# Conv taps and modulation rows shared out anew between the stages of a layer, and the last expert's activations turned on TensorE

## The reference

```python
mod = c_act @ w_ada[l] + b_ada[l]              # six rows of 1024
shift1, scale1, gate1, shift2, scale2, gate2 = split(mod, 6)
h = rms_norm(x) * (1 + scale1) + shift1
proj = h @ w_in[l]
attn_out = attention of 4 heads, 1024 x 1024 softmax each
conv_out = silu(layer_norm(conv of 31 taps over 512 channels (a * sigmoid(g))))
x = x + gate1 * (concat(attn_out, conv_out) @ w_out[l])
h2 = rms_norm(x) * (1 + scale2) + shift2
x = x + gate2 * expert_choice_ffn(h2)          # 16 experts, each takes 128 tokens
```

## Time and profile before

| | |
|---|---|
| median of 3 runs | 4063.68 us (4060.52 to 4064.96) |
| profiled execution | 4063.72 us, its span 4061.9 us |
| TensorE busy | 3778.4 us, 93% of the span |
| VectorE busy | 2656.0 us, 65% |
| ScalarE, GpSimd busy | 22%, 13% |
| mean granted TensorE clock | 0.971 of full speed |

### The profile page before, as it was taken

The page is one execution under the profiler, slowest core; times in us unless marked ns, Lnnn a source line. Parts: engine busy times, 40 slices in busy tenths (PEclk is TensorE's granted clock), DMA queues, the critical chain, the costliest instruction groups (busy, mean ns, idle before and its releaser), DMA issues. The chain is left out here.

```text
span 4061.9 us, 41680 instructions
## 1 busy us (share of the span) xinstructions
PE 3778.4 (93%) x16116; PEld 1723.8 (42%) x16116; DVE 2656.0 (65%) x3557; ACT 901.9 (22%) x1736; POOL 546.1 (13%) x415
## 2 busy tenths in 40 slices
PE   6989995999997998996999999799988999999998
PEld 3444442333333444443333333344476444444443
DVE  6779737888885588966688888445443253333676
ACT  2244321111111234421211111233243110000000
POOL 2000002121111000001111110000020022222541
PEclk8999997999998999998999999899998999999999
DMA  8210327999995631055799998311010111111454
GB/s 300 82 42 1 123 80 286 350 348 348 351 347 181 228 103 42 1 194 211 277 350 357 342 355 329 104 36 37 16 45 17 75 46 52 42 42 42 176 202 166
DMA packets 186964, 682.50 MB, mean 168 GB/s; under 512 B 16656, under 2 KB 80784, under 8 KB 137616
## 3 DMA queue, kind: packets, MB, share of 16 engines
q1 hardware_dynamic: 177264, 646.27, 42.4%
q0 software_dynamic: 9504, 33.56, 3.4%
HBM read 637.83 MB, written 41.94 MB: 167 GB/s over the span
## 5 line engine op out<-in xcount | busy, mean ns | idle before, releaser
L1724 PE MATMUL ps<-w_raw,h_act 128*64 128x512 f32 x2048 | 456.0, 598 | 6.2 <-ACT h_act L1829 6.2
L1777 PE MATMUL ps<-w_down,h_act 128*128 128x512 f32 x960 | 417.2, 592 | 0.6 <-DVE h_act L1945 0.6
L1724 PE MATMUL ps<-w_t,h_act 128*64 128x512 f32 x1536 | 342.0, 594 | 0.0
L3437 PE MATMUL ps<-h_act,arena_two 128*128 128x512 f32 x704 | 313.2, 592 | 1.8 <-ACT h_act L455 0.9
L983 DVE SCALAR_TENSOR_TENSOR y<-y,par_one 128x1024 f32<-128x1024 f32 x240 | 307.2, 1280 | 2.6
L1724 PEld LDWEIGHTS ps<-w_raw,h_act 128*64 128x64 f32 x2048 | 148.7, 138 | 300.1 <-issue 300.1
L1777 PEld LDWEIGHTS ps<-w_down,h_act 128*128 128x128 f32 x960 | 180.1, 190 | 217.6 <-issue 215.2
L3437 PE MATMUL ps<-arena_two 128*128 128x512 f32 x528 | 237.4, 592 | 0.0
L1945 DVE STREAM_TRANSPOSE h_act<-h_act 32x256 f32<-32x256 f32 x512 | 223.2, 436 | 20.6
L2279 PE MATMUL ps<-h_act,arena_two 128*128 128x512 f32 x544 | 235.4, 593 | 1.0 <-DVE h_act L466 1.0
L650 PE MATMUL ps<-h_act,arena_a 128*128 128x512 f32 x512 | 221.6, 593 | 4.5 <-DVE h_act L466 2.0
(11 more groups left out here) (487 smaller groups left out, 5830.8 us busy)
## 6 DMA issues: line engine op xcount, KB each, us to landing
w_raw<-in_w_gate SPq DMA_DIRECT2D x128, 1024.0 KB, 7.4
w_raw<-in_w_up SPq DMA_DIRECT2D x128, 1024.0 KB, 9.9
w_down<-in_w_down SPq DMA_DIRECT2D x128, 1024.0 KB, 8.2
arena_two<-in_ffn_w_down SPq DMA_DIRECT2D x44, 1024.0 KB, 4.9
arena_two<-in_ffn_w_up SPq DMA_DIRECT2D x22, 1024.0 KB, 5.1
arena_b<-in_w_ada SPq DMA_DIRECT2D x32, 512.0 KB, 5.3
arena_b<-in_w_ada_T SPq DMA_DIRECT2D x32, 512.0 KB, 4.4
arena_two<-in_w_in SPq DMA_DIRECT2D x21, 512.0 KB, 3.9
```

Source lines behind the costliest of these rows:

```text
L1724: last = nc.tensor.matmul(out[w * TOK:(w + 1) * TOK, :], left[:, k, :], right[:, w, k, :], start=begins and k == 0, stop=k == KH1 - 1, ski ...
L1777: last = nc.tensor.matmul(ps[:, 4 + i, :], hidT[:, k * P:(k + 1) * P], down[:, c, k % 2, i * HALF:(i + 1) * HALF], start=(k == 0), stop=(k ...
L3437: last = nc.tensor.matmul(ps[:, q % 8, :], left[:, k, :], right[k], start=k == 0, stop=k == KH - 1)
```

## The change

- Layer 1's rows 3 and 4 (16 pieces) are no longer computed in layer 1's `mix_one`, but in layer 0's `out_projection_one`, whose number of pieces rises from 16 to 32. There `fills["rows"]` is 14 for both layers; in layer 0 it was 16, and the other places of `fills`, 18 pieces in all, were not reached. Layer 1's `mix_one` keeps the gate rows of its own and of the second block (32 pieces in place of 48).
- In `mix_one` of both layers the fills ahead of the attention units have 92 places in place of 80. With 32 pieces these hold 60 taps (before: 48 in layer 0, 32 in layer 1).
- In the attention units the first five take one tap each, and the others `left // (N_UNITS - u)`, with six taps held back until after the last unit.
- In the last expert of each layer VectorE doesn't turn the activations. TensorE turns them with eight 128 x 128 transposes in two groups of four into two PSUM banks, ScalarE copies each bank to `hidT`, and `last_down` takes k = 4 to 7 first.

```diff
+FIRST_UNITS, LAST_TAPS = 5, 6
...
                 gate(0)
-                fill(20)
+                fill(21)
                 gate(1)
+                fill(5)
                 for t in range(QT):
                     scale_latents(t)
-                    fill(3)
+                    fill(3 + t % 2)
...
-                fill(16)
+                fill(18)
                 gate(2)
                 fill(20)
...
-                    left = n_taps - done[0]
-                    some = -(-left // (N_UNITS - u))
+                    left = n_taps - LAST_TAPS - done[0]
+                    some = 1 if u < FIRST_UNITS else left // (N_UNITS - u)
                     tap_some(min(1, some))
...
                     tap_some(max(0, some - 1))
+                tap_some(LAST_TAPS)
...
-    fills = {"rows": 16 if l == 0 else 14, ("added", 0): 2, ("added", 1): 2, ("scaled", 0): 2, ("scaled", 1): 2, ("scored", 3): 2,
+    fills = {"rows": 14, ("added", 0): 2, ("added", 1): 2, ("scaled", 0): 2, ("scaled", 1): 2, ("scored", 3): 2,
...
+LAST_ORDER = (4, 5, 6, 7, 0, 1, 2, 3)
...
+                def turn_last(part):
+                    pe.wait_ge(hid_parts, 4 * final + 3 + part)
+                    for n in range(4):
+                        k = LAST_ORDER[4 * part + n]
+                        last = nc.tensor.transpose(ps[:, 6 + part, n * P:(n + 1) * P], hid[:, k * P:(k + 1) * P], core.c("ident", P))
+                    last.then_inc(last_turned, 1)
+
                 def last_down():
-                    pe.wait_ge(hidT_kept, 16 * N_EXP)
                     pe.wait_ge(ye_kept, final)
                     for i in range(2):
-                        for k in range(KD):
+                        for n, k in enumerate(LAST_ORDER):
+                            pe.wait_ge(last_kept, n // 4 + 1)
...
+                for part in range(2):
+                    turn_last(part)
                 last_down()
...
+                act.wait_ge(down_used, PER * final)
+                for part in range(2):
+                    act.wait_ge(last_turned, part + 1)
+                    at = LAST_ORDER[4 * part] * P
+                    nc.scalar.activation(hidT[:, at:at + HALF], ps[:, 6 + part, :], ACT.Copy).then_inc(last_kept, 1)
...
-                    turn_hidden(e, 0)
+                    if e < final:
+                        turn_hidden(e, 0)
...
-                    turn_hidden(e, 1)
                     if e == final:
                         break
+                    turn_hidden(e, 1)
...
-        gates = [(l, 2), (l, 5)] + ([(DEPTH, 2), (DEPTH, 5)] if l + 1 == DEPTH else [])
-        mod = Modulation(core, a, gates + [(l, 3), (l, 4)], [ar.x[:, i, :] for i in range(4)], [ar.x[:, 4 + i, :] for i in range(4)],
+        second = [(l, 3), (l, 4)] if l == 0 else [(DEPTH, 2), (DEPTH, 5)]
+        mod = Modulation(core, a, [(l, 2), (l, 5)] + second, [ar.x[:, i, :] for i in range(4)], [ar.x[:, 4 + i, :] for i in range(4)],
...
-            rows = [(l + 1, 0), (l + 1, 1)] + ([(DEPTH, 3), (DEPTH, 4)] if l + 1 == DEPTH else [])
+            rows = [(l + 1, v) for v in (0, 1, 3, 4)]
```

More of the change, by code:

```diff
@@ L1583, in experts @@
     first_half, second = slice(0, HALF), slice(HALF, 2 * HALF)
-    (xe0, xe1, xe_turned, xeT_kept, hidT_kept,
+    (xe0, xe1, xe_turned, xeT_kept, hidT_kept, last_turned, last_kept,
      m1_done, m2_done, m6_done, m5_done, m7_done, m3_done, m4_done, down_used,
@@ L1589, in experts @@
      ye_kept, scattered, last_made, eights, indexed, replaced, placed, lists_turned, lists_kept, turned_back, chosen) = together.take(
-        "xe0", "xe1", "xe_turned", "xeT_kept", "hidT_kept",
+        "xe0", "xe1", "xe_turned", "xeT_kept", "hidT_kept", "last_turned", "last_kept",
         "m1_done", "m2_done", "m6_done", "m5_done", "m7_done", "m3_done", "m4_done", "down_used",
@@ L1790, in last_down @@
                                                     down[:, k // 2, k % 2, i * HALF:(i + 1) * HALF],
-                                                    start=(k == 0), stop=(k == KD - 1))
+                                                    start=(n == 0), stop=(n == KD - 1))
                         last.then_inc(last_made, 1)
```

## The result

The changed kernel takes 4014.2 us, the median of four runs (4010.22 to 4025.53), against 4063.15 us (4060.52 to 4064.96, four runs) before. The ratio is 0.9885 with an interval of 0.9864 to 0.9905: 48.9 us less, where 48.9 were worked out.

What follows compares the result with a forecast made beforehand. VectorE was taken to bound units with three taps, TensorE those with fewer and the output projection; the last expert was a chain. Layer terms of -18.7 and -30.2 us, against 4063.72, gave 4015 us; range 4009 to 4023.

Steps and rivals of the forecast that it cites:

- Attention units: First to last peak reduction: 164.1 us at TensorE's pace, saving 13.4 us in layer 0 and 24.5 in layer 1.
- The six taps behind: After the last attention unit: 7.9 us of taps hidden in VectorE's 9.99 us wait, cost nothing, 2.1 us cover left.
- `gate(3)`: Ahead of the attention: this gate comes later, costing 2.2 us in layer 0 and 1.8 in layer 1.
- Cost 1.8 us: Layer 1 ahead of the attention: net delay from a later `gate(3)`, less two `keep`s found made.
- The clock ahead of the units: TensorE's longer gap before the preparation could cost clock: 0 to 1.7 us more per layer, left out of the sum.
- Output projection: Layer 0: 18 more late pieces covered by TensorE, cost 0, bounds -1.4 to +0.3 us.
- Last expert: From `m4` to the end of the product, each layer: 7.5 us less, bounds 4.9 to 7.7.
- The term of 2.5 us: Last product's first half: 6.8 in place of 9.35 us if TensorE's clock holds.
- The rival of the clock as now: Last product: clock falls despite the transposes, 2.5 or 5 us less gain, 4017.5 to 4020 us; chance 0.16.
- the slow row: 20 transposes by themselves took 4.26 us, 0.21 each against 0.13 in a steady unit; read as agreeing with the rule.
- The sum: Whole kernel: -18.7 us in layer 0 and -30.2 in layer 1, together -48.9, giving 4014.8, said as 4015.
- The range: Whole kernel's time: 4009 to 4023 us, held at about 0.85.

Runs made afterwards that it cites:

- the repeat of the changed kernel: The changed kernel measured once more, unaltered, for comparison on one chip; 4017.27 us, ratio 0.9894.
- with `gate(3)` early: Changed kernel, five taps moved from ahead of `gate(3)`: two behind the kept gate rows, two before the first unit, one to the end; 4010.56 us.
- 48 transposes: Changed kernel with 48 further transposes between the last expert's two groups of transposes; one run, 4019.97 us.
- seven matmuls: Changed kernel with seven `keep_awake` matmuls between the last expert's two groups of transposes; one run, 4033.09 us.
- the rows alone: Kernel before with only layer 1's rows 3 and 4 moved to layer 0's output projection, taps in their places; 4053.56 us, ratio 0.9979.
- by the clock alone: Kernel before with seven unused 128 x 512 matmuls in TensorE's idle time ahead of the last product; 4057.72 us, ratio 0.9990.
- 144 of them: Changed kernel with 144 further transposes between the last expert's two groups of transposes; one run, 4048.5 us.

## Why the prediction was right

*Attention units.* Predicted 164.1 us in both layers, measured 164.07, and 164.07 to 164.09 in every kernel that has no unit with three taps. Without any taps it is still 164.07, so TensorE's pace is the bound, as the sum had it. That the saving agrees in each layer to 0.1 us hangs on the trace compared with (177.49 or 179.2 us in layer 0, 188.64 or 187.00 in layer 1); the sum of both, 38.0, doesn't.

*The six taps behind.* Predicted at nothing, measured 0.00 and -0.01 us, with 2.06 us left in the trace. As cover these were counted too high: 12 taps show about 1 us of it, and the seventh tap already costs 0.35.

*`gate(3)`.* In layer 0 the term was 2.2 us; `gate(3)` came 2.35 us later and TensorE's restart 2.34. In layer 1 `gate(3)` was put 3.8 us later and came 4.31, and the keeps behind it saved 1.8 us as described. The net term was "Cost 1.8 us" and measured 2.5. The term was mis-sized by 0.7 us: `gate(3)` was put 0.5 us too early, and the saving behind it, 1.8, was put at 2.0.

*The clock ahead of the units.* The bound of 0 to 1.7 us more in each layer was crossed in layer 1's profile. From restart to first peak took 59.41 us where the earlier trace rows of before had 57.62 to come (1491.54 to 1549.16). Six microseconds of it, TensorE alone (length, busy time, granted clock, DMA share, GB/s):

```profile
1524.00:1530.00 6.00, 5.57 (x24) 0.50 0.97 365
```

The clock is at 1.2 GHz there, in 24 transposes that follow 0.95 and 1.50 us of idle time; over the whole way from restart to first peak its mean is 0.94, and was 1.00 in the kernel before. The place at which it is paid changes: layer 0 went the other way (59.32 against 60.51 us), in the repeat of the changed kernel the two layers took 60.01 and 58.76, and with `gate(3)` early 57.58 and 57.57, the shortest seen. In three other profiles with the same program ahead of the units (last expert as before, 48 transposes, seven matmuls), layer 1 pays before the restart, in TensorE's last sums of the gate rows. The first row is the changed kernel's, the second that of the one with the last expert as before:

```profile
1469.77 3.70 PE L258 MATMUL ps<-arena_b,con 128*128 128x512 f32 x8 [1.90 <-DVE y L1009]
```

```profile
1478.07 5.40 PE L258 MATMUL ps<-arena_b,con 128*128 128x512 f32 x8 [1.90 <-DVE y L1009]
```

The restart is then 7.98 us behind `gate(3)` in place of 6.29, so that the saving by the `keep`s is gone, and in two of the three the rest takes 57.6 us. A count that holds both places runs from `gate(0)` to the first peak reduction. In the profiles with the fills of before it is 197.3 to 200.1 us in layer 0 (four) and 199.7 to 200.1 in layer 1 (three); in the eight with the changed fills, this one among them, 201.3 to 202.8 and 202.3 to 205.0. By the means the change costs 3.5 and 3.9 us there, where 2.2 and 1.8 were put; in layer 1 six of the eight lie above the bound of 1.8 + 1.7 us. This is the term that the sum had too small, by 3.4 us in all, and it is so in most profiles and not in this one alone. The prediction named this price and took it at nothing in its sum.

*Output projection.* Predicted 0, at most +0.3. One profile of the changed kernel has +0.66 us in both layers, above that bound, yet the rows alone, with the same pieces, have none, and the repeat has +0.66 in layer 0 and 0 in layer 1. Over all profiles it wavered between 146.7 and 149.4 us. So the pieces are hidden, and 0 stands. TensorE is busy 1.2 us longer in these 147.33 us, at 0.97 in place of 0.98 of the clock, but the repeat's layer 1 took 146.89 at 0.97 too; that the clock makes the rest is not shown.

*Last expert.* Predicted 7.5 us a layer, 5.2 for the start and 2.5 for the clock, a little rounded down. Measured 5.18 at the start, and 2.1 and 2.2 at the first half (2.0 and 2.1 by the clock alone, in the kernel before): 7.3 and 7.4 in place of 7.5. The term of 2.5 us took the first half to 6.8, as long as the second; it stays 7.14. The prediction had compared unlike counts: the second half is counted from one scaling to the next, the first from its first matmul, and so holds some 0.34 us more at any clock. From the start of the stage to the scaling it is 6.90 and 7.23 us less in this profile, and 7.4 by the means of all profiles with either last expert.

*The transposes and the clock.* The rival of the clock as now is refuted. The Trainium skill ("TensorE: Matmul & The Clock Gate", Part 4) says that a transpose does not count as TensorE being busy in the way a matmul does, which had made the sum 4020. Here the measurement decides against it for transposes issued one behind the other: 48 and 144 of them, 128 x 128 in fp32, left the clock at 1.00. The trace names them MATMUL, so it doesn't say whether these are the form that the page means. The slow ones, the 20 of the earlier trace rows and the 24 in layer 1's preparation, also run one behind the other, but behind idle times of 0.95 and 1.50 us with only eight transposes between, and at a low clock: 0.60 on average in the 20, and in the changed kernel 0.50 from 1524.00, before the first of the 24 at 1524.43. Among the 20 it comes back: the mean is 0.54 from 265 to 267 us, 0.61 to 269 and 1.00 from there, with nothing but transposes since 265.00. So the slow row, which the prediction read as agreeing with the rule, does not bear it out. Whether the idle times alone made the clock fall there was not tried by itself.

*The sum.* -18.7 and -30.2 us were worked out; the trace has -18.8 and -27.4. In layer 0 the agreement is one of the sum and not of its terms: 1.2 us less from `gate(3)` to the first peak and 0.4 less ahead of `gate(0)` stand against 0.7 more in the output projection, 0.6 in the last expert, and 0.2 and 0.1 in smaller terms. The 2.8 us missing in layer 1 are the late start (0.7), the clock in the preparation (1.8), the output projection (0.7) and the last expert (0.2), less 0.5 in the stage ahead of `gate(0)` and 0.1 in the units. The two measurements of the changed kernel gave 48.9 and 41.9 us; the interval of the one is 38.6 to 55.3 us, that of the other 36.1 to 49.5. By the means over the profiles, 38.0 us in the units and 14.8 in the last experts less 7.4 ahead of the units, the change is worth some 45 us, between the two. That the median fell to within 1 us of the forecast is therefore luck. The range held both medians and seven of the eight executions.

## What to carry to other kernels

Where a filler engine runs beside a pacing one, count its work per unit against the pacing engine's and move just enough out to fall below it: here two taps a unit fit and three don't, and the last 58 taps are free. Put what is moved behind a gate that another engine waits for, not ahead of it, as the version with the early `gate(3)` shows: 6.7 us faster, with TensorE restarting 2.9 and 2.2 us earlier. At a chain's end, count the idle time of TensorE twice, once as time and once as clock behind it: 5.2 and 2.1 us here. And allow for the same price wherever a change makes a gap of TensorE longer, as ahead of the units here, where it was left out of the sum.

## What the hardware showed that was not expected

Transposes in fp32 on TensorE, back to back, take 15.88 / 144 = 0.11 us each at full clock, half of the 0.21 in the earlier trace rows, where the granted clock was 0.60. A stage of 5301 small matmuls that no kernel of this study changed took from 547.2 to 559.7 us, a swing of 12.5 us, a quarter of the whole effect; TensorE's busy time in it goes from 506.7 to 517.8 us, with a mean granted clock of 0.97 in the shortest and 0.95 in the longest, and what starts it was not settled.
